# Experts of a grouped top-2 MoE: pairs in rounds of 64 rows against single experts in blocks of 32 rows

## The reference, cut to what matters

```python
N_EXPERTS, N_GROUPS, TOP_K, D_EXPERT = 32, 4, 2, 512

def moe(tokens, w_router, b_router, w1, w3, w2):
    scores = jax.nn.sigmoid(tokens @ w_router)
    sel = scores + b_router
    grp = lax.top_k(sel.reshape(T, N_GROUPS, per), 2)[0].sum(-1)
    g_idx = jnp.argmax(grp, axis=-1)
    ...
    _, e_idx = lax.top_k(jnp.where(in_group, sel, -jnp.inf), TOP_K)
    gate = take_along_axis(scores, e_idx); gate = gate / gate.sum(-1)
    ...
    def expert_block(xb, e):
        return (jax.nn.silu(xb @ w1[e]) * (xb @ w3[e])) @ w2[e]
    ...
    return einsum('tk,tkd->td', gate, y[dest_assign])
```

## Time and profile before

| | us |
|---|---|
| median of 3 runs (lowest, highest) | 3429.77 (3427.25, 3431.69) |
| the profiled execution's own time | 3428.47 |
| its span, first to last instruction | 3426.3 |
| mean granted TensorE clock over the span | 0.949 |
| TensorE / VectorE / ScalarE / POOL busy | 3128.9 / 1422.9 / 835.0 / 260.7 |
| bytes moved by DMA | 676 MB, of them 564 on SyncE's queue |
| weight DMAs of the ring | 768 of 512 KB, 15.1 us from issue to landing |
| stores of expert outputs | 53 of 512 KB |
| zero fill of `y_dram` | 2 of 14080 KB, 65.8 us each |
| first routing step of layer 0, first weight load, first expert product, last store's issue | 1143.2, 1164.5, 1193.7, 1822.4 |
| the same in layer 1, from the first weight load | 2765.8, 2792.0, 3377.3 |

### The profile page before, as it was taken

How to read it: one execution, slowest core, us unless ns; L and a number is a source line. 1 busy time by engine, 2 the same in 40 slices (tenths; PEclk the granted TensorE clock), 3 DMA queues, 4 the chain that set the end, 5 groups by cost and what they waited for, 6 DMA issues and landing times. The chain is left out here.

```text
span 3426.3 us, 48079 instructions
## 1 busy us (share of the span) xinstructions
PE 3128.9 (91%) x17203; PEld 1776.6 (52%) x17203; DVE 1422.9 (42%) x4218; ACT 835.0 (24%) x1611; POOL 260.7 (8%) x324
## 2 busy tenths in 40 slices
PE   6999976899999699999996999899999969999983
PEld 3666645645555444444443455477775534444441
DVE  2333346665474411111113688666665431111113
ACT  1111113466511000000002344355551100000001
POOL 0000004400060000000000000000002000000001
PEclk8999988899999699999998999999999979999996
DMA  9700075200052779999964222100003187899998
GB/s 345 297 25 24 13 292 165 80 1 1 1 167 80 272 292 392 411 411 411 381 239 171 80 86 74 68 1 1 1 1 131 68 332 283 326 411 411 411 410 328
DMA packets 217637, 676.22 MB, mean 197 GB/s; under 512 B 24004, under 2 KB 36468, under 8 KB 217460
## 3 DMA queue, kind: packets, MB, share of 16 engines
q1 hardware_dynamic: 188212, 564.31, 42.8%
q0 software_dynamic: 20176, 76.55, 6.0%
q10 hardware_dynamic: 9072, 33.03, 2.4%
HBM read 579.32 MB, written 94.50 MB: 197 GB/s over the span
## 5 line engine op out<-in xcount | busy, mean ns | idle before, releaser
L2678 PE MATMUL ps_u<-w_ring,work 128*64 128x256 f32 x3392 | 381.3, 382 | 11.1 <-DMA w_ring<-in_w 11.1
L2666 PE MATMUL ps_g<-w_ring,work 128*64 128x512 f32 x1696 | 377.2, 596 | 5.8 <-DMA w_ring<-in_w 5.8
L2697 PE MATMUL ps_y<-w_ring,work 128*64 128x512 f32 x1696 | 375.6, 595 | 0.0
L2678 PEld LDWEIGHTS ps_u<-w_ring,work 128*64 128x64 f32 x3392 | 244.5, 138 | 161.9 <-issue 32.9
L1705 PE MATMUL of_ps_r<-of_w,cat 128*128 128x512 f32 (+1 forms) x608 | 257.7, 580 | 3.0 <-ACT cat L1788 3.0
L2666 PEld LDWEIGHTS ps_g<-w_ring,work 128*64 128x64 f32 x1696 | 121.8, 138 | 251.5 <-issue 240.2
L423 PE MATMUL ps_r<-w,hT 128*128 128x512 f32 (+1 forms) x640 | 249.4, 546 | 1.5 <-ACT hT L482 1.5
L2697 PEld LDWEIGHTS ps_y<-w_ring,work 128*64 128x64 f32 x1696 | 117.1, 137 | 220.6 <-issue 220.6
L2752 DVE SCALAR_TENSOR_TENSOR work<-work,ps_g 128x512 f32<-128x512 f32 x53 | 36.4, 687 | 366.1 <-ACT work L2730 366.1
L1432 PE MATMUL mo_ps_o<-mo_w,mo_cT 128*128 128x512 f32 x416 | 186.1, 599 | 1.4 <-DMA mo_w<-in_e_w_out 0.9
L1705 PEld LDWEIGHTS of_ps_r<-of_w,cat 128*128 128x128 f32 x608 | 115.7, 194 | 127.1 <-issue 123.4
(11 more groups left out here) (511 smaller groups left out, 4334.6 us busy)
## 6 DMA issues: line engine op xcount, KB each, us to landing
w_ring<-in_w SPq DMA_DIRECT2D x768, 512.0 KB, 15.1
y_dram<-zeros POOLq DMA_DIRECT2D x2, 14080.0 KB, 65.8
y_dram<-work ACTq DMA_DIRECT2D x53, 512.0 KB, 6.7
ml_staging<-in_w_ada SPq DMA_DIRECT2D x9, 2048.0 KB, 11.9
w_ring<-in_w_ada SPq DMA_DIRECT2D x6, 2048.0 KB, 13.3
ml_spare<-in_w_ada SPq DMA_DIRECT2D x5, 2048.0 KB, 13.4
ml_arena<-ml_rows SPq DMA_DIRECT2D x40, 256.0 KB, 4.4
f_dram<-mo_f SPq DMA_DIRECT2D x18, 512.0 KB, 2.8
```

What stands on the lines that cost most here:

```text
L2666: mm = pe.matmul(ps_g[rows, :], xT[:, k, rows], weight(k // 2)[:, h, (k % 2) * DE:(k % 2 + 1) * DE], start=k == 0, stop=k == KD - 1)
L2678: mm = pe.matmul(ps_u[rows, f, 0:256], xT[:, k, rows], weight(4 + k // 2)[:, h, at:at + 256], start=k == 0, stop=k == KD - 1)
L2697: mm = pe.matmul(ps_y[rows, half, :], hT[:, k, rows], weight(8 + k)[:, h, half * 512:(half + 1) * 512], start=k == 0, stop=k == 3)
```

## The change

The experts are no longer paired. Each expert takes its rows in blocks of 32 (`UNIT`), at least two per expert. A block uses four column groups of 32 with the same 32 tokens: the 1024 model columns are cut into four quarters, and column group n computes another part of the output's columns.

- **Up and gate** are one product: for a chunk (now 256 rows of w1 and the same of w3), each group n takes 128 columns of w1 and 128 of w3, as one moving operand of 256 columns. 4 chunks x 2 x 4 groups. A block's h is 128 partitions x 128, and it is transposed by one transpose instead of four; a block's tokens by two transposes of 128 x 128 (each gathered row is a quarter of a token, four partitions groups hold the quarters).
- **Second matrix**: four groups of 256 output columns, 2 chunks x 2 x 4 groups. It is done one block later: in TensorE's order, up of block b, transpose of h of block b-1, transposes of x of block b+1, second matrix of block b-1.
- **Ring**: 6 chunks per expert, 20 slots as before, each chunk still two DMAs of 512 KB.
- **Gather**: 128 rows of 1 KB per block into one of four buffers, each with its own semaphore; POOL copies a landed buffer to `xs`, which TensorE transposes, and gathers four blocks ahead.
- **Output**: 128 x 256, copied by ScalarE alone to one of four buffers with a semaphore each, stored as 32 rows of 4 KB in 1 KB pieces. ScalarE's loop does four blocks a turn, so it and POOL can run past the last block, and TensorE adds to their semaphores at the end. VectorE no longer copies tokens or outputs.
- **Routing**: the order comes from rank with three steps in place of eleven; the table has 32 entries; the place in `y_dram` needs no arithmetic on bit fields; `high` has 149 columns and `low` 32, and the list is made in four column groups.
- `y_dram` shrinks from 7040 to 4608 rows, and so does its zero fill.

```diff
-NPAIR = NE // 2
-MAXB = 2 * T // HALF + NPAIR - 1
-LISTW = MAXB + 1
+UNIT = 32
+MAXB = 2 * T // UNIT + 2 * NE - 3
+AHEAD = 4
+LISTW = MAXB + 2 * AHEAD
+YB = -(-(MAXB + AHEAD - 1) * UNIT // P)
-PER_PAIR = 12
+CHUNKS = 6
...
+        pe.wait_ge(low_in, 1)
         for a in range(2 * nt):
-            mm = pe.matmul(ps_l[:, 0:LISTW], low[:, a * P:(a + 1) * P], high[:, a * LISTW:(a + 1) * LISTW], start=a == 0, stop=a == 2 * nt - 1)
+            for q in range(P // UNIT):
+                mm = pe.matmul(ps_l[q * UNIT:(q + 1) * UNIT, 0:LISTW], low[:, a, :], high[:, a * LISTW:(a + 1) * LISTW], start=a == 0, stop=a == 2 * nt - 1)
...
+        dve.tensor_scalar(E_, rk, -2.0, float(2 * NE - 2), ALU.mult, ALU.add).then_inc(*c.up())
+        dve.tensor_scalar(at, rk, 2.0, 1.0, ALU.mult, ALU.add).then_inc(*c.up())
+        own()
+        dve.tensor_tensor(at, at, E_, ALU.min).then_inc(*c.up())
...
+        dve.tensor_scalar(rounds[:, :], units[:, :], 2.0, None, ALU.max).then_inc(*c.up())
...
 def load_chunk(sp, A, layer, R, e, u, c):
+    slot = (u * CHUNKS + c) % RING
     for h in range(2):
+        if c < 4:
+            src = A[("w1", "w3")[h]][layer, bass.ds(e, 1), c * 256:(c + 1) * 256, :].rearrange("o (p k) n -> p (o k n)", p=P)
         else:
+            at = (2 * (c - 4) + h) * P
+            src = A["w2"][layer, bass.ds(e, 1), at:at + P, :].rearrange("o p n -> p (o n)")
...
+                sp.wait_ge(w_used, last * CHUNKS + (2, 3, 4, 5, 12, 13)[chunk])
...
+    # POOL
+        with pool.Fori(0, fours) as i:
+            for at in range(AHEAD):
+                pool.wait_ge(gathered[at], i * 16 + 16)
+                pool.wait_ge(x_turned, i * AHEAD + (at + 1))
+                pool.sem_inc(xs_free, 1)
+                pool.tensor_copy(xs, xg[:, at * 256:(at + 1) * 256]).then_inc(x_ready, 1)
+                pool.wait_ge(x_ready, i * AHEAD + (at + 1))
+                gather(i * AHEAD + (AHEAD + at), at)
...
+        def up(u, gb):
+            pe.wait_ge(x_out, gb + 1)
+            pe.wait_ge(h_ready, gb + 1)
+            for c in range(4):
+                take(u, c)
+                w = R.w[:, (u * CHUNKS + c) % RING, :, :]
+                for kk in range(2):
+                    for n in range(QU):
+                        rows = slice(n * UNIT, (n + 1) * UNIT)
+                        at = kk * DE + n * P
+                        mm = pe.matmul(ps_h[rows, :], xT[:, kk, c * UNIT:(c + 1) * UNIT], w[:, :, at:at + P], start=c == 0 and kk == 0, stop=c == 3 and kk == 1)
...
+        def down(u, now):
+            pe.wait_ge(y_out, now)
+            pe.wait_ge(hT_ready, now)
+            for i in range(2):
+                take(u, 4 + i)
+                ...
+                        mm = pe.matmul(ps_y[n * UNIT:(n + 1) * UNIT, :], hT[:, k * UNIT:(k + 1) * UNIT], w[:, kk, n * 256:(n + 1) * 256], start=k == 0, stop=k == 3)
...
+        for u in range(NE):
+            start, more = span_of(pe, u)
+            if u:
+                up(u, start)
+                turn_h(start)
+                turn_x(start + 1)
+                down(u - 1, start)
+            with pe.Fori(0, more) as b:
+                gb = start + b + 1
+                up(u, gb)
+                turn_h(gb)
+                turn_x(gb + 1)
+                down(u, gb)
...
+    # ScalarE
+        def store(now, b, uses):
+            act.wait_ge(y_done, now)
+            act.wait_ge(y_st[b], uses * 16 + 16)
+            act.copy(y[:, b, :], ps_y).then_inc(y_out, 1)
+            act.wait_ge(y_out, now + 1)
+            act.dma_start(R.y_dram[bass.ds(now * UNIT + -UNIT, UNIT), :].rearrange("t (n d) -> n t d", n=QU), y[:, b, :]).then_inc(y_st[b], 16)
...
+    # VectorE
+        def hidden(gb):
+            dve.wait_ge(th_done, gb + 1)
+            dve.scalar_tensor_tensor(out=hr, in0=th, scalar=1.0, in1=ps_h[:, 0:P], op0=ALU.add, op1=ALU.mult).then_inc(th_used, 1)
+            dve.wait_ge(th_used, gb + 2)
+            dve.scalar_tensor_tensor(out=hr, in0=hr, scalar=0.5, in1=ps_h[:, P:2 * P], op0=ALU.mult, op1=ALU.mult).then_inc(h_ready, 1)
+        def copy_h(now):
+            dve.wait_ge(h_turned, now)
+            dve.tensor_copy(hT, ps_t).then_inc(hT_ready, 1)
```

More of the change, by code:

```diff
@@ L2230, in route @@
     n, m = nt * NE, nt * NG
-    PIECE = 5
     def s(name):
@@ L2570, in experts @@
[L2570 to L2577 removed]
+    QU = P // UNIT
@@ new lines, in experts, with inside @@
+    gathered = [s(f"gathered{at}") for at in range(AHEAD)]
+    up_done, th_done, th_used, h_ready, h_turned, hT_ready = s("up_done"), s("th_done"), s("th_used"), s("h_ready"), s("h_turned"), s("hT_ready")
+    y_done, y_out = s("y_done"), s("y_out")
+    y_st = [s(f"y_st{b}") for b in range(AHEAD)]
+    def total_rounds(eng):
+        return eng.value_load(R.table[0:1, NE:NE + 1], min_val=2 * NE, max_val=MAXB)
+    def inside(v, low, high):
+        return nc.s_assert_within(v, low, high, skip_runtime_bounds_check_because="MAXB rounds at most, two at least for an expert")
@@ L2600, in _ @@
         if layer:
-            sp.wait_ge(w_used, last * PER_PAIR + (R.x_chunks[-1] + 2))
+            start, more = span_of(sp, NE - 3)
+            sp.wait_ge(w_used, (start + more) * CHUNKS + 3)
             for n in range(NTL):
@@ L2707, in _ @@
         pe.wait_ge(R.tabled, 1)
-        for pair in range(NPAIR):
-            entry = pe.value_load(R.table[0:1, pair:pair + 1], min_val=0, max_val=32 * 64 - 1)
-            start = nc.s_assert_within(entry // 32, 0, MAXB - NPAIR, skip_runtime_bounds_check_because="MAXB rounds at most, one each for the pairs") + pair
-            rounds = nc.s_assert_within(entry % 32 + 1, 1, 32, skip_runtime_bounds_check_because="each pair has a round")
-            with pe.Fori(0, rounds) as b:
-                round_of(pair, nc.s_assert_within(start + b, 0, MAXB - 1, skip_runtime_bounds_check_because="MAXB rounds at most"))
+        up(0, 0)
+        turn_x(1)
+        pe.sem_inc(w_used, 2)
+        for u in range(NE):
[6 more added lines that the diff above has]
+            with pe.Fori(0, more) as b:
+                gb = inside(start + b + 1, 1, MAXB - 1)
+                up(u, gb)
+                turn_h(gb)
+                turn_x(gb + 1)
+                down(u, gb)
+        total = total_rounds(pe)
+        turn_h(total)
+        down(NE - 1, total)
+        pe.wait_ge(y_done, total)
+        for turned in (x_turned, up_done, y_done):
+            pe.sem_inc(turned, AHEAD)
     @block.scalar
```

348 lines of the change are left out of this document (124 added, 224 removed).

## The result

The changed kernel takes **3472.55 us** (median of 4 runs, 3471.27 to 3477.43); the kernel before, run beside it, 3428.51. The ratio is **1.0132, 95% interval 1.0115 to 1.0150**: slower, where the forecast was faster (3393 us). The profiled execution took 3473.57 us, its span is 3471.9.

A forecast was written before the change was run, and what follows sets the result against it. TensorE bounds layer 0's expert stage and mostly layer 1's, which ends bound by weights. Layer 0 -32.5, layer 1 -6, routing +2, tails +1 make -35.5 us: 3393 us from 3428.5; range 3370 to 3520.

The forecast's parts named there:

- Blocks and TensorE: Both expert stages: 98 and 89 blocks of 32 rows, each 6.05 us on TensorE with four column groups side by side.
- Rivals 1, 2 and 3: Each block: longer per-block costs, near 3525 us (0.17); loads in turn, near 3660 (0.10); shape changes emptying TensorE, near 3457 (0.05).
- rival 3: Each change between column groups and full array empties TensorE, 0.27 us at each of two; near 3457 us; chance 0.05.
- The DMA side: Weights plus block gathers and stores: layer 0 585 us against TensorE's 593; layer 1 576 against 538, so DMA-bound.
- rival 5: Block gathers and stores: a 1 KB packet costs 37 ns, a quarter of a 4 KB one; 3384 us; chance 0.10.
- Stage 0, -32.5: Layer 0's expert stage: 98 blocks of 6.05 us, 593 us against 625.5, so 32.5 us less.
- Layer 1, -6: Layer 1's expert stage, becoming DMA-bound: 6 us less, or 15 less at 37 ns a packet.
- 13 us idle on a full ring: Layer 1, heavy experts first: weight queue idle 13 us, some 16 with the second matrix's chunks held a block longer.
- the traffic of 89 blocks: Layer 1's gathers and stores: 256 packets per block at 61 ns, 0.98 us a block, 87 us added to 489 of weights.
- Routing, +2: Routing before the expert products: fewer steps but larger compares and list; 2 us more, between -3 and +8.
- Tails, +1: After the expert stages: one or two surplus rounds of ScalarE (ACT), 1 us more.
- Rival 4: Layer 1's stage: 1 KB rows cost over 61 ns or expert order starves the ring; 20 to 40 us more; chance 0.15.

## Why the prediction was wrong

**Blocks and TensorE: right.** 98 + 89 blocks, 6.08 us each against my 6.05; four column groups do run side by side at 256 columns. Rivals 1, 2 and 3 fell by the timeline: a block of 6.08 us has no room for the 0.27 us at each of two changes of shape that rival 3 would add, nor for loads in turn (7.7 us).

**The DMA side: the step that failed.** It said "256 packets per block: 0.59 to 0.98 us. I take the measured 61 ns." Its count and its price were wrong, both to the safe side. 128 of the 256 were the gather's, which moves 32 packets of 4 KB. And the 61 ns belong to no 1 KB packet. The sizes in the stretch that they came from:

```profile
DMA packets 5881, 5.87 MB, mean 147 GB/s; under 512 B 347, under 2 KB 3931, under 8 KB 5877
```

347 closing packets, 3584 of 512 bytes and 1946 of 2 KB have a mean of 1.0 KB; by the records they take 9, 27 and 89 ns (medians). A 1 KB packet took 46 ns here beside 159 for one of 4 KB: 16% dearer per byte, between rival 5's 7% and its 65%. A block's traffic is so 0.70 us of a mean engine (5.9% + 5.8% of 100 us over 16.7 blocks), under my 0.98.

What failed is the spreading. The step spread the 128 packets of a store over 16 engines, as the price per share of 16 engines does. They run on 4, so a block costs each of these 32 x 46 ns = 1.47 us, and 0.35 for the gather, where I had at most 0.98 in all. Over 98 blocks the slow engines need 667 us for layer 0 (measured 657) while TensorE needs 29.6 us to its first product and 596 for the blocks. So "Layer 0: 489 + 96 = 585 us against 593 of TensorE" is the time of no engine: by the same sum it is 667 on the four with the stores and 488 + 98 x 0.35 = 522 on the twelve without.

The Trainium skill states the rule (DMA: Bandwidth & Descriptors, Why a DMA increments its semaphore by 16 and not by 1): the number of engines is the largest one up to 16 that divides the slowest dimensions of both sides, and for transfers issued by ScalarE these are the lowest-numbered. The runs agree in number (132, 144, 192 packets a block) and in that two such stores share their engines (3772 us); that these are the lowest-numbered, no view shows. I had read the store's pattern in the diff and its size in bytes, and not its slowest dimension.

**Stage 0, -32.5: right but for that step.** With the store spread it is 598.9 us, 29.8 less than before's 628.7. In the changed kernel, -1.4.

**Layer 1, -6: the same.** With the store spread 577.3, that is -8.0. In the changed kernel +36.7. That the queue and the order would set it was right, but two terms missed in opposite directions, and that they cancelled in good part is luck: the "13 us idle on a full ring" was undersized, since spreading the order gave 30.6 us, and the traffic of 89 blocks was oversized by 0.98 - 0.70 = 0.28 us each, 25 us.

**Routing, +2: wrong in sign, small.** From its first step to the first product it takes 49.9 us where it took 50.4, and 45.6 where it took 46.2 in layer 1. The 6.8 us before it are in no term of the prediction. **Tails, +1: undersized.** They gave +4.7 and +7.9; I counted one or two surplus rounds, rightly, and priced them at a fraction of the 4.3 us that each costs; why it is so much is settled only in part (above).

**Rival 4** had the place (stage 1, 3413 to 3437) and two causes: the place was half right, since stage 0 lost its whole gain too. "Rows of 1 KB cost more than 61 ns under load" was wrong; that the order starves the ring was right in itself, 30.6 us, but not the reason for the miss. That stage 0 would wait for weights stood among the signs against the forecast, and is what came.

Repaired in that one step the kernel takes 3396.8, where the forecast was 3393. That is closer than its terms deserve. Of the 32.1 us between the two spans, the stages give 29.8 and 8.0, and the part before the routing 6.5, which nobody forecast; the tails take back 10.7 where I had 1, and the rest is under 2 us.

## What to carry to other kernels

Read a DMA's slowest dimension on both sides before its bytes: a small transfer with 4 there is four times its size on four engines, and every large transfer that is waited for as a whole waits for those four. The signs here were a rate under the saturated one with a share near it, waits for loads that should have had slack, and in a queue's packet count the number of closing packets per transfer. When two resources are within a few per cent of each other, ask also in which order the work is laid out, since a ring that is full early lacks those bytes at the end.

## What the runs showed of the hardware

- Sixteen engines' mean hides four full ones (full by the sum of 667 us against 657): share 0.97 to 0.99 and 368 to 371 GB/s with TensorE starved for 69 us, against 1.03 and 408 late in layer 1 with the same bytes spread.
- A store queue that is held back stops the engine that issues: 0.59 us per issue at the median, up to 11.7, with the store on two engines.
- Work that is balanced over all engines costs in full as soon as a few bind: leaving out the gathers, 5.8% of the share, gave 56 us (1.6%).
- Four issues in place of one cost nothing here (3396.8 against 3397.2 us), though each is 0.32 us of ScalarE at the median; the single issue of the changed kernel was 0.56.
- Packets of 4 bytes, 512 bytes, 1 KB, 2 KB and 4 KB take 9, 27, 46, 89 and 159 ns at the median in the traces: about 8 ns each and 19 ns for every 512 bytes (an estimate from these five, within 6%). Indirect gathers of 1 KB rows moved as 4 KB packets.
